# Value steps, page turns and sample scores set between the index pairs of a hybrid decoder layer

## Chip, cores and metric

The kernel runs on one core of one Trainium2 chip. Times are device microseconds of that core. The figure that counts is the median over repeated runs; a profile shows one execution of its own.

## The reference, cut to what matters

One layer of a hybrid model works on a prompt of 1024 tokens and on 8 sample sequences of 4 new tokens each (1056 rows in all, float32). It projects the rows, runs a state-space branch and a sparse attention, mixes both and applies a feed-forward network. The change touches three parts of it:

```
qi, ki, wi : index queries (8 heads of 64), index keys (64), head weights
v          : values (512 columns)
score[t, s] = sum over h of relu(qi[t, h] . ki[s] * 64**-0.5) * wi[t, h] * 8**-0.5
prompt : keys s are the prompt's own 1024 index keys, causal; the 256 best are kept
sample : keys s are 512 past keys from the paged cache (4 pages of 128 rows
         for each of the 8 sequences) and the 4 new ones; the 129 best are kept
```

The first 256 prompt rows keep all their keys, so scores are needed for the prompt's row tiles 2 to 7 and for the sample rows only.

## The kernel before, in words

The program is a sequence of blocks. In a block each engine has its own list of instructions, in an order written out by hand, and they meet through semaphores; a barrier of all engines ends a block. The block in question is the second half of the first one ("s2" semaphores). It ends at 249 us; the block behind it (s3) is called block 3 below.

Projections use float32 numbers split in a high and a low part, with three products each (`split_mm`, L139 to L141). A weight chunk of 1024 x 256 is loaded by SyncE (`load_w`, L199), its high part is written by ScalarE (`split_high`, L205), its low part by GpSimd (`split_low`, L211). There are two chunk buffers, so chunk n+2 can be loaded when the products of chunk n are done. Chunk 5 holds the first 256 value columns, chunk 6 the other 256 (used at the start of block 3), chunk 7 the first gates.

**The index ring.** `UNITS` are the 48 pairs of a row tile i (2 to 7) and a head h. PE works on two units at a time (a pair, 24 in all), one in each half of its rows, over 128 (i + 1) keys (L1016). Their sums go to three slots of two PSUM banks (banks 0 to 5). ScalarE takes each unit through a ReLU into one of two buffers R (L627), VectorE multiplies it with the head's weight and adds it to the tile's scores (L859; the first head of a tile by L854 and L855). A pair may start on PE when the first ReLU of the pair before it is done (`relu_done >= u - 1`); a ReLU waits for the accumulation two units earlier.

**Value columns.** `project_v(n)` computes 128 rows of 256 value columns: 8 steps over the contraction, 3 products each, 24 products in one run. Tile 0 stands ahead of the ring. Tiles 1 to 8 stand behind pairs 2, 4, ..., 16, a whole tile at a time (`FILL`), in banks 6 and 7 by turns. ScalarE copies a tile out (`v_cols`, L617), SyncE stores it.

**Sample scores.** Behind the last pair, PE turns the index pages of one sequence (4 transposes of 128 rows, `pages_T`, L1031), ScalarE or VectorE copies the turned keys and the four new keys to SBUF (L639, L640, L872, L873), and after four sequences PE multiplies them with the sample queries (`sample_units`, L1039); this twice. ScalarE applies the ReLU (L646), PE multiplies with a matrix of head weights that sums over heads (L1052), VectorE copies the scores out (L876, L877).

**SyncE's queue.** All loads and stores are issued by SyncE, in this order: 9 stores of index keys, the load of chunk 5, 32 page loads (L431), the store of the sample head weights (L435), the load of chunk 6, two stores of the state-space kernels (L441), then for each value tile its store (L445) and, for the first four, 8 tiny loads of head weights (L450), the load of chunk 7, and when all index products are done the 8 loads of Uc (L457). Uc is the input of the state-space branch for block 3, 128 partitions x 32 groups x 145 columns, read back from DRAM in rows of 580 bytes; it lies over the index queries `qiT`, which is why it waits for the index products. At its end SyncE waits for the stores of this block, the value stores among them, but not for Uc or weight chunks. PE waits for Uc in block 3, after three value tiles. The first thing that ScalarE does in block 3 is the split of chunk 7.

**ScalarE ahead of the ring** copies the sample queries (L608) and the value tile 0. The split of chunk 6 stands behind unit 20, and GpSimd's part follows it.

Of the kernel before, what the change touches and what calls it, by code (L numbers as in the profile page):

```python
# [17 lines left out]
P = 128  # L18
# [77 lines left out]
def hybrid_kernel(nc, a, outs):  # L96
# [5 lines left out]
    def sem(name):  # L102
        return nc.alloc_semaphore(name=name)
# [181 lines left out]
    qiT = view(36568, 4, T)  # L285
    pg = view(31896, NB, NPG, HD)
    Rb = view(31896, NG, LS)
# [5 lines left out]
    kbT = view(50600, BG, LS)  # L293
# [13 lines left out]
    FILL = [-1] + [5 + 4 * n for n in range(NT - 1)]  # L307
# [5 lines left out]
    with nc.Block() as block:  # L313
# [48 lines left out]
        pT_ev = [sem("s2_pT_ev_act"), sem("s2_pT_ev_dve")]  # L362
        sqk_done = sem("s2_sqk")
        srelu_done = sem("s2_srelu")
# [7 lines left out]
        def _(sp):  # L372
# [55 lines left out]
            for b in range(NB):  # L428
                for j in range(NPG):
                    page = sp.value_load(pt[0:1, b * NPG + j:b * NPG + j + 1], min_val=0, max_val=n_phys - 1)  # L430
                    sp.dma_start(pg[:, b, j, :],  # L431
                                 a["cache_kidx"].rearrange("l n r d -> (l n) r d")[bass.ds(page, 1)]
                                 .rearrange("n r d -> (n r) d")).then_inc(pg_in[b // BG], 16)
            sp.wait_ge(wsc_done, 1)
            sp.dma_start(wi_dram, wsc[0:NB * NS, NT - 1, :]).then_inc(wi_st, 16)  # L435
            sp.wait_ge(mm_done, 15)
            load_w(sp, 6)
            sp.wait_ge(wi_st, 16)
            sp.wait_ge(kern_ev, 10)
            for z in range(2):  # L440
                sp.dma_start(kern_dram[:, GP * z:GP * (z + 1), :],  # L441
                             Kb[32 * z:32 * z + GI].rearrange("i g c -> i g c")).then_inc(kern_st, 16)
            for n in range(NT):
                sp.wait_ge(v_out, n + 1)
# [8 lines left out]
            sp.wait_ge(unit_mm, len(UNITS))  # L453
            sp.wait_ge(qiS_done, 2)
            sp.wait_ge(u_st, 64)
            for t in range(L):
                sp.dma_start(Uc[GI * t:GI * (t + 1), :, :],  # L457
                             u_dram.rearrange("(g i) t c -> t i g c", i=GI)[L - 1 - t]).then_inc(uc_in, 16)
# [34 lines left out]
        def _(act):  # L493
# [113 lines left out]
            for half in range(2):  # L607
                nc.scalar.activation(  # L608
                    qiS[0:64].rearrange("p b (m h) t -> p h m b t", h=2)[:, half],
                    qiT[64 * half:64 * half + 64, :, SEQ:T].rearrange("p m (b t) -> p m b t", t=NS),  # L610
                    ACT.Copy).then_inc(qiS_done, 1)

            def v_cols(n):
                act.wait_ge(v_mm, n + 1)
                if n >= 2:
                    act.wait_ge(v_st[n % 2], 16 * (n // 2))
                nc.scalar.activation(vst1[own(n), n % 2, :], psum[own(n), 6 + n % 2, 0:WC], ACT.Copy).then_inc(v_out, 1)  # L617

            act.wait_ge(tabs, 1)
            v_cols(0)  # L620
            act.wait_ge(kern_ev, 10)
            for u, (i, h) in enumerate(UNITS):
                act.wait_ge(unit_mm, u + 1)
                if u >= 2:
                    act.wait_ge(acc_done, u - 1)
                nk_ = keys_of(i)
                nc.scalar.activation(R[:, u % 2, 0:nk_],  # L627
                                     psum[:, 2 * (u % 3):2 * (u % 3) + 2, :].rearrange("p a b -> p (a b)")[:, 0:nk_],
                                     ACT.Relu, scale=HD ** -0.5).then_inc(relu_done, 1)
                if u == 20:  # L630
                    split_high(act, 6)
                if u in FILL:
                    v_cols(FILL.index(u))
            act.wait_ge(acc_done, len(UNITS))
            for b in range(0, NB, 2):
                act.wait_ge(pT_done, b + 1)
                if b >= BG:
                    act.wait_ge(sqk_done, 1)
                nc.scalar.activation(kbT[0:HD, b % BG, 0:PAST], psum[0:HD, b % 2, :], ACT.Copy)  # L639
                nc.scalar.activation(kbT[0:HD, b % BG, PAST:LS], kiT[0:HD, SEQ + NS * b:SEQ + NS * (b + 1)],  # L640
                                     ACT.Copy).then_inc(pT_ev[0], 1)
                if b == BG + 2:
                    for g in range(NG):
                        act.wait_ge(sqk_done, g + 1)
                        qk = psum[:, 2 + 2 * g:4 + 2 * g, :].rearrange("p a b -> p (a b)")[:, 0:LS]
                        nc.scalar.activation(Rb[:, g, :], qk, ACT.Relu, scale=HD ** -0.5).then_inc(srelu_done, 1)  # L646

        @block.vector
        def _(dve):
# [196 lines left out]
            dve.wait_ge(wsc_done, 1)  # L846
            for u, (i, h) in enumerate(UNITS):
                dve.wait_ge(relu_done, u + 1)
# [11 lines left out]
            dve.wait_ge(wcol_in, 16 * BG * H)  # L860
            for g in range(NG):
                for b in range(BG):
                    rb = slice(HR * b, HR * (b + 1))
                    v.tensor_scalar(wsel[rb, g, NS * (BG * g + b):NS * (BG * g + b + 1)], Et[rb, :], wcol[rb, g:g + 1], None,
                                    ALU.mult).then_inc(sel_done, 1)
            for b in range(1, NB, 2):
                dve.wait_ge(pT_done, b + 1)
                if b == 1:
                    dve.wait_ge(acc_done, len(UNITS))
                if b >= BG:  # L870
                    dve.wait_ge(sqk_done, 1)
                v.tensor_copy(kbT[0:HD, b % BG, 0:PAST], psum[0:HD, b % 2, :])  # L872
                v.tensor_copy(kbT[0:HD, b % BG, PAST:LS], kiT[0:HD, SEQ + NS * b:SEQ + NS * (b + 1)]).then_inc(pT_ev[1], 1)  # L873
            dve.wait_ge(sacc_done, 1)
            ssc = scores(NT - 1)
            link(v.tensor_copy(ssc, psum[0:rs, 6:8, :].rearrange("p a b -> p (a b)")[:, 0:LS]))  # L876
# [3 lines left out]
        def _(pe):  # L880
# [111 lines left out]
            def project_v(n):  # L992
                if n == 0:
                    pe.wait_ge(w_lo_done, 6)
                if n >= 2:
                    pe.wait_ge(v_out, n - 1)
                for k in range(KD):
                    last = split_mm(psum[:, 6 + n % 2, 0:WC], h_parts(k, tok0(n), tok0(n) + P), w_parts(5, k, 0, WC),
                                    k == 0, k == KD - 1)
                last.then_inc(v_mm, 1)  # L1000

            pe.wait_ge(kw_ev, 2)
            project_v(0)
# [3 lines left out]
            for u in range(0, len(UNITS), 2):  # L1007
                i, h = UNITS[u]
                nk_ = keys_of(i)
                if u >= 2:  # L1010
                    pe.wait_ge(relu_done, u - 1)
# [8 lines left out]
                if u + 1 in FILL:  # L1020
                    project_v(FILL.index(u + 1))
            pe.wait_ge(relu_done, len(UNITS))
            pe.wait_ge(v_out, NT)
            pe.wait_ge(qiS_done, 2)

            def pages_T(b):
                pe.wait_ge(pg_in[b // BG], 16 * BG * NPG)
                if b >= 2:
                    pe.wait_ge(pT_ev[b % 2], b // 2)
                for j in range(NPG):  # L1030
                    last = tr(psum[0:HD, b % 2, j * P:(j + 1) * P], pg[:, b, j, :], ident)  # L1031
                last.then_inc(pT_done, 1)

            def sample_units(g):
                for z in range(2):
                    pe.wait_ge(pT_ev[z], BG // 2 * (g + 1))
                for n0, n1 in ((0, 512), (512, LS)):
                    for b in range(BG):
                        last = mm(psum[HR * b:HR * (b + 1), 2 + 2 * g + n0 // 512, 0:n1 - n0],  # L1039
                                  qiS[0:HD, BG * g + b].rearrange("p h t -> p (h t)"), kbT[0:HD, b, n0:n1],  # L1040
                                  start=True, stop=True, tile_position=(0, HR * b))
                last.then_inc(sqk_done, 1)

            for g in range(NG):
                for b in range(BG * g, BG * (g + 1)):
                    pages_T(b)
                sample_units(g)
            pe.wait_ge(sel_done, NB)
            for g in range(NG):
                pe.wait_ge(srelu_done, g + 1)  # L1050
                for n0, n1 in ((0, 512), (512, LS)):
                    last = mm(psum[0:NB * NS, 6 + n0 // 512, 0:n1 - n0], wsel[:, g, :], Rb[:, g, n0:n1],  # L1052
                              start=(g == 0), stop=(g == NG - 1))
            last.then_inc(sacc_done, 1)
# [7 lines left out]
        wcol_in, ki_st, mm_done, ev_done, kw_T, kw_ev, wsc_done, qiS_done, unit_mm, relu_done, acc_done, pT_done, *pT_ev,  # L1062
# [2547 lines left out]
```

## Time and profile before

| | |
|---|---|
| median of 3 runs | 1759.78 us (1758.2 to 1760.35) |
| the profiled execution | 1756.8 us |
| its span | 1755.0 us, mean granted clock 0.981 |
| PE busy | 1646.0 us, 94% |
| VectorE (DVE) busy | 1149.8 us, 66% |
| ScalarE (ACT) busy | 738.5 us, 42% |
| GpSimd (POOL) busy | 641.3 us, 37% |

Shares are of the span. PEld, in the rows, is PE's loading of weights, which overlaps its products. A granted clock of 1.00 is 2.4 GHz, 0.50 is 1.2 GHz. The index ring takes 157 to 231 us of the span, the sample scores 231 to 248. Names such as view_at stand for most tiles, since they are views of one arena; lines tell them apart.

### The profile page before, as it was taken

How to read it: one execution, taken by the hardware profiler on the slowest of the kernel's cores; microseconds unless marked ns; L12 is line 12 of the kernel's file. 1: busy time of each engine (PE TensorE's matmuls, PEld its weight loads, DVE VectorE, ACT ScalarE, POOL GpSimd, SP SyncE). 2: the span in 40 equal slices, each digit the busy share in tenths (PEclk: the TensorE clock that was granted, in tenths of full speed). 3: DMA queues.
4: the chain of work that ended last, by engine and by line, in shares of the span. 5: the costliest groups of instructions: out<-in, count | busy, mean ns of one | idle time of the engine just before them, and what ended most of it. 6: DMA issues, size and time to landing. Idle time of an engine off the chain costs nothing.

```text
span 1755.0 us, 31434 instructions
## 1 busy us (share of the span) xinstructions
PE 1646.0 (94%) x12368; PEld 1510.6 (86%) x12368; DVE 1149.8 (66%) x1946; ACT 738.5 (42%) x1333; POOL 641.3 (37%) x382
## 2 busy tenths in 40 slices
PE   6999879999999998997899999899999999999998
PEld 6997559999999955554699999899999899999998
DVE  5684666998875528872343169565555578998786
ACT  6423547547334435453322335444444433333342
POOL 6121116312212000001544330444444476777792
PEclk9999989999999989999899999999999989999999
DMA  6322151224961114006552433564444464453422
GB/s 164 107 80 59 41 67 53 94 90 119 155 170 40 42 53 146 1 1 201 187 163 90 135 90 107 178 190 166 141 141 145 168 234 160 164 168 135 136 88 99
DMA packets 170197, 209.11 MB, mean 119 GB/s; under 512 B 27410, under 2 KB 114418, under 8 KB 170002
## 3 DMA queue, kind: packets, MB, share of 16 engines
q1 hardware_dynamic: 170050, 207.10, 39.3%
q8 instruction: 98, 1.61, 0.4%
q14 instruction: 49, 0.40, 0.1%
HBM read 148.28 MB, written 58.78 MB: 118 GB/s over the span
## 4 chain that ended last, share of the span: by engine, by line
PE 30%; POOL 9%; DVE 4%; DMA 3%; issue 2%; ACT 2%; SPq 1%; DVEq 0%; ACTq 0%; POOLq 0%
PE psum L139 10%; PE psum L141 10%; PE psum L140 10%; POOL da_lo L3262 5%; DMA view_at<-hid_dram 3%; POOL view_at L3271 1%; ACT da_hi L3138 1%; POOL view_at L3278 1%; POOL view_at L3281 1%; POOL view_at L3274 1%; DVE view_at L3342 1%; SPq L2724 1%; DVE b_lo L3348 1%; PE psum L2863 0%; ACT db_hi L3133 0%
## 5 line engine op out<-in xcount | busy, mean ns | idle before, releaser
L139 PE MATMUL psum<-db_hi,da_hi 128*128 128x264 f32 x896 | 256.6, 286 | 13.9 <-DVE view_at L3458 8.1
L139 PE MATMUL psum<-b_hi,ua_hi 128*128 128x264 f32 x896 | 257.0, 287 | 9.9 <-DVE psum L3406 3.4
L140 PE MATMUL psum<-db_lo,da_hi 128*128 128x264 f32 x896 | 256.4, 286 | 0.0
L141 PE MATMUL psum<-db_hi,da_lo 128*128 128x264 f32 x896 | 256.4, 286 | 0.0
L141 PE MATMUL psum<-b_hi,ua_lo 128*128 128x264 f32 x896 | 256.0, 286 | 0.0
L140 PE MATMUL psum<-b_lo,ua_hi 128*128 128x264 f32 x896 | 255.4, 285 | 0.0
L3258 POOL TENSOR_TENSOR ua_lo<-view_at,ua_hi 128x512 fp32r<-128x512 f32 x99 | 137.3, 1391 | 189.2 <-ACT ua_hi L3067 189.1
L211 POOL TENSOR_TENSOR w_lo<-view_at,w_hi 128x2048 fp32r<-128x2048 f32 (+1 forms) x18 | 81.9, 4548 | 323.7 <-ACT w_hi L205 323.6
L139 PE MATMUL psum<-h_hi,w_hi 128*128 128x352 f32 x600 | 195.1, 325 | 1.3 <-POOL w_lo L211 1.3
L140 PE MATMUL psum<-h_lo,w_hi 128*128 128x352 f32 x600 | 192.7, 321 | 0.0
L141 PE MATMUL psum<-h_hi,w_lo 128*128 128x352 f32 x600 | 192.6, 321 | 0.0
L139 PEld LDWEIGHTS psum<-db_hi,da_hi 128*128 128x128 f32 x896 | 170.2, 190 | 15.9 <-issue 8.5
L3262 POOL TENSOR_TENSOR da_lo<-view_at,da_hi 128x1024 fp32r<-128x1024 f32 x56 | 149.6, 2689 | 93.6 <-ACT da_hi L3138 93.6
L139 PEld LDWEIGHTS psum<-b_hi,ua_hi 128*128 128x128 f32 x896 | 170.0, 190 | 11.2 <-issue 11.1
L141 PEld LDWEIGHTS psum<-b_hi,ua_lo 128*128 128x128 f32 x896 | 170.1, 190 | 0.0
L140 PEld LDWEIGHTS psum<-b_lo,ua_hi 128*128 128x128 f32 x896 | 170.0, 190 | 0.0
L140 PEld LDWEIGHTS psum<-db_lo,da_hi 128*128 128x128 f32 x896 | 169.5, 189 | 0.0
L141 PEld LDWEIGHTS psum<-db_hi,da_lo 128*128 128x128 f32 x896 | 169.4, 189 | 0.0
L3473 DVE TENSOR_TENSOR view_at<-psum,view_at 128x528 f32<-128x528 f32 x204 | 135.7, 698 | 31.9 <-PE psum L141 29.6
L3437 DVE TENSOR_TENSOR db_lo<-view_at,db_hi 128x1056 fp32r<-128x1056 f32 x56 | 118.1, 2108 | 23.1 <-ACT db_hi L3133 22.9
L139 PE MATMUL psum<-w_hi,h_hi 128*128 128x256 f32 x432 | 126.1, 292 | 3.0 <-PEq L1064 2.3
L140 PE MATMUL psum<-w_lo,h_hi 128*128 128x256 f32 x432 | 122.7, 284 | 0.0
(398 smaller groups left out, 3978.2 us busy)
## 6 DMA issues: line engine op xcount, KB each, us to landing
hid_dram<-view_at SPq DMA_DIRECT2D x112, 264.0 KB, 2.1
view_at<-hid_dram SPq DMA_DIRECT2D x56, 528.0 KB, 3.8
view_at<-w_in SPq DMA_DIRECT2D x18, 1024.0 KB, 5.4
view_at<-w_up SPq DMA_DIRECT2D x16, 1024.0 KB, 6.3
view_at<-w_down SPq DMA_DIRECT2D x32, 512.0 KB, 5.7
gate_dram<-view_at SPq DMA_DIRECT2D x48, 176.0 KB, 2.0
view_at<-gate_dram SPq DMA_DIRECT2D x16, 528.0 KB, 4.5
view_at<-cache_k SPq DMA_DIRECT2D x32, 256.0 KB, 3.5
```

The lines of the kernel that those rows point to most:

```text
L139: nc.tensor.matmul(out, lhs[0], rhs[0], start=start, stop=False, skip_group_check=more)
L140: nc.tensor.matmul(out, lhs[0], rhs[1], start=False, stop=False, skip_group_check=more)
L141: return nc.tensor.matmul(out, lhs[1], rhs[0], start=False, stop=stop, skip_group_check=more)
L211: nc.gpsimd.tensor_tensor(w_low[n % 2][:, :, 0:width], w_raw[n % 2][:, :, 0:width], f32(w_high[n % 2][:, :, 0:width]), ALU.subtract).then_ ...
L2724: sp.dma_start(raw_d[d % 2][:, k0::2, cols], w_dn[d][:, k0::2, cols]).then_inc(raw_d_in[j], 16)
L3138: nc.scalar.activation(dah[n % SLOTS], src_d(n), ACT.Copy).then_inc(da_hi, 1)
L3258: tt(slot_u(n)[1], src_u(n), f32(slot_u(n)[0]), ALU.subtract).then_inc(ua_lo, 1)
L3262: tt(dal[n % SLOTS], src_d(n), f32(dah[n % SLOTS]), ALU.subtract).then_inc(da_lo, 1)
L3271: tt(s_d[0], w21, w22, ALU.add).then_inc(sd_done, 1)
L3274: tt(s_d[1], s_d[0], w11, ALU.subtract).then_inc(sd_done, 1)
L3437: v.tensor_tensor(dbl[n % SLOTS], raw_b[n % 3], f32(dbh[n % SLOTS]), ALU.subtract).then_inc(db_lo, 1)
L3473: v.tensor_tensor(two(to), pair(mt), two(to), ALU.add).then_inc(drained, 1)
```

## The change

- Value tiles 1 to 8 are no longer done a tile at a time. Their 64 steps are dealt out behind the pairs: 3, 3, 2 steps in turn behind pairs 0 to 20, then 2, 2, 0 and 4. They use bank 6 alone, so the first step of a tile waits until ScalarE has copied the tile before it.
- The pages of one sequence are turned behind each of pairs 3, 5, ..., 17, in bank 7, and ScalarE alone copies them out, to places that are free during the ring. The order of the sequences is 0, 4, 1, 5, 2, 6, 3, 7. The second of two groups goes to the other half of the partitions.
- The sample units are pair 23 of a ring of 25 pairs: they use the ring's slots and ScalarE's place in it. The four new keys of a sequence are read from `kiT`, not from a copy. The prompt units behind them are shifted by two slots (`ring_of`). The sums over heads follow the last prompt pair. VectorE's eight weight products (`select_weights`) stand ahead of its last two units.
- The page loads of the second group, and ahead of them the store of the sample head weights and the load of chunk 6, change places in SyncE's queue. `split_high(act, 6)` stands ahead of value tile 0; the split in the ring is gone. The sample queries are copied in four instructions.
- Uc is loaded in two parts: groups 0 to 13 when the products of pair 21 are done (they lie over the query heads 0 to 3, which no later pair reads), groups 14 to 31 when the last pair's are. Both parts stand in the queue ahead of the last value tile's store and of the load of chunk 7. Block 3 waits for both.

The diff, cut to its core:

```
+    PB = [g * BG + s for s in range(BG) for g in range(NG)]
-    FILL = [-1] + [5 + 4 * n for n in range(NT - 1)]
+    PAIRS = len(UNITS) // 2 + 1
+    SAMPLE = PAIRS - 2
+        take = (3, 3, 2)[pair % 3] if pair < 21 else (2, 2, 0, 4)[pair - 21]
+    UC_EARLY = 2 * T // UC
+    SUMS = 2 * ((2 * SAMPLE + 1) % 3)
+    PAGE_OF_PAIR = {3 + 2 * n: n for n in range(NB)}
...
 SyncE
-            for b in range(NB):
+            for n, b in enumerate(PB):
+                if n == BG:
+                    sp.wait_ge(wsc_done, 1)
+                    sp.dma_start(wi_dram, wsc[0:NB * NS, NT - 1, :]).then_inc(wi_st, 16)
+                    sp.wait_ge(mm_done, 15)
+                    load_w(sp, 6)
...
             for n in range(NT):
+                if n == NT - 1:
+                    sp.wait_ge(qiS_done, 4)
+                    sp.wait_ge(u_st, 64)
+                    sp.wait_ge(unit_mm, 2 * (SAMPLE - 1))
+                    load_uc(0, UC_EARLY)
+                    sp.wait_ge(unit_mm, 2 * PAIRS)
+                    load_uc(UC_EARLY, G)
                 sp.wait_ge(v_out, n + 1)
                 sp.dma_start(rows(nv, n)[:, 0:WC], vst1[own(n), n % 2, :]).then_inc(v_st[n % 2], 16)
...
             load_w(sp, 7)
-            sp.wait_ge(unit_mm, len(UNITS))
-            for t in range(L):
-                sp.dma_start(Uc[GI * t:GI * (t + 1), :, :],
...
 ScalarE
+            split_high(act, 6)
             act.wait_ge(tabs, 1)
             v_cols(0)
...
-                if u == 20:
-                    split_high(act, 6)
+                for n, k in V_OF_PAIR[pair]:
+                    if k == KD - 1:
+                        v_cols(n)
+                if pair in PAGE_OF_PAIR:
+                    page_out(PAGE_OF_PAIR[pair])
...
 PE
+            def project_v(n, k):
+                if n >= 1 and k == 0:
+                    pe.wait_ge(v_out, n)
...
+            for pair in range(PAIRS):
+                if pair == SAMPLE:
+                    sample_units()
+                else:
+                    prompt_units(2 * pair if pair < SAMPLE else 2 * pair - 2)
+                if pair == PAIRS - 1:
+                    sample_sums()
+                for n, k in V_OF_PAIR[pair]:
+                    project_v(n, k)
+                if pair in PAGE_OF_PAIR:
+                    pages_T(PAGE_OF_PAIR[pair])
...
-            pe.wait_ge(uc_in, 16 * L)
+            pe.wait_ge(uc_in, 2 * 16 * L)
```

## Rows read from the trace of the kernel before

**Rows 1.** Stretches: length, busy us of each engine, granted clock, DMA share, GB/s.
```profile
157.00:231.00 74.00, 58.96 (x356) 36.88 (x355) 47.08 (x54) 39.36 (x58) 4.52 (x1) 1.00 0.17 51
...
230.80:249.10 18.30, 11.53 (x72) 5.79 (x72) 7.30 (x20) 3.83 (x10) 0.00 (x0) 0.72 1.20 115
```

**Rows 2.** PE in order of time: start us, us, line, operation, count [idle before].
```profile
157.06 0.92 PE L1016 MATMUL psum<-view_at,view_at 64*128 64x384 f32 x4
...
160.10 0.92 PE L1016 MATMUL psum<-view_at,view_at 64*128 64x384 f32 x4 [0.57 <-ACT view_at L627]
...
160.94 0.39 PE L139 MATMUL psum<-w_hi,h_hi 128*128 128x256 f32 x1
...
163.98 0.92 PE L1016 MATMUL psum<-view_at,view_at 64*128 64x384 f32 x4
...
190.24 1.56 PE L1016 MATMUL psum<-view_at,view_at 64*128 64x512 f32 x8 [0.79 <-ACT view_at L627]
...
195.03 1.56 PE L1016 MATMUL psum<-view_at,view_at 64*128 64x512 f32 x8 [0.19 <-ACT view_at L627]
...
223.73 1.99 PE L1016 MATMUL psum<-view_at,view_at 64*128 64x512 f32 x8 [1.11 <-ACT view_at L627]
226.82 1.99 PE L1016 MATMUL psum<-view_at,view_at 64*128 64x512 f32 x8 [1.11 <-ACT view_at L627]
```

**Rows 3.** Groups by shape, 157 to 232 us: busy us, mean ns, idle before.
```profile
L859 DVE SCALAR_TENSOR_TENSOR view_at<-view_at,view_at,view_at 128x1024 f32<-128x1024 f32 x7 | 9.0, 1284 | 2.0 <-ACT view_at L627 1.6
...
L627 ACT ACTIVATE view_at<-psum 128x1024 f32<-128x1024 f32 x8 | 7.8, 1021 | 4.7 <-PE psum L1016 4.7
```

**Rows 4.** All engines in order of time, the sample tail and the next block's start.
```profile
230.83 1.06 PE L1031 MATMUL psum<-view_at,view_at 128*64 128x128 f32 x8 [2.02 <-ACT view_at L627]
...
243.81 1.10 PE L1039 MATMUL psum<-view_at,view_at 64*32 64x512 f32 x16 [0.94 <-DVE view_at L873]
...
244.84 2.00 PE L1052 MATMUL psum<-view_at,view_at 128*32 128x512 f32 x8
...
247.60 0.15 DVE L877 TENSOR_TENSOR view_at<-view_at,view_at 32x4 f32<-32x4 f32 x1
...
249.15 1.91 ACT L205 ACTIVATE w_hi<-view_at 128x2048 fp32r<-128x2048 f32 x1 [3.55 <-PEq L1064]
```

**Rows 5.** SyncE's queue in order of time: start us, us of issuing, line, transfer, count.
```profile
150.57 7.99 SPq L431 DMA_DIRECT2D view_at<-cache_kidx  x8
...
228.88 10.25 SPq L457 DMA_DIRECT2D view_at<-u_dram  x8
```

**Rows 6.** Busy time by stretch, just after the next block has started.
```profile
250.00:252.00 2.00, 2.00 (x11) 2.00 (x11) 1.63 (x14) 1.06 (x1) 0.79 (x1) 0.50 0.28 28
```

**Rows 7.** Timeline around a gate store; medians to landing (page, part 6).
```profile
455.89 1.94 SPq L1204 DMA_DIRECT2D gate_dram<-view_at  x1
...
466.93 0.47 ACT L1346 ACTIVATE view_at<-psum 128x352 f32<-128x352 f32 x1 [7.66 <-DMA gate_dram<-view_at]
...
view_at<-w_in SPq DMA_DIRECT2D x18, 1024.0 KB, 5.4
...
gate_dram<-view_at SPq DMA_DIRECT2D x48, 176.0 KB, 2.0
```

**Rows 8.** GpSimd's weight splits and VectorE beside them, in order of time.
```profile
154.11 1.28 DVE L838 COPY view_at<-psum 16x512 f32<-16x512 f32 x2 [0.47 <-PE psum L987]
...
155.42 0.41 DVE L844 TENSOR_TENSOR view_at<-view_at,view_at 16x256 f32<-16x256 f32 x1
...
187.88 4.52 POOL L211 TENSOR_TENSOR w_lo<-view_at,w_hi 128x2048 fp32r<-128x2048 f32 x1 [46.80 <-ACT w_hi L205]
188.43 4.66 DVE L859 SCALAR_TENSOR_TENSOR view_at<-view_at,view_at,view_at 128x640 f32<-128x640 f32 x1 [1.65 <-ACT view_at L627]
...
251.21 4.61 POOL L211 TENSOR_TENSOR w_lo<-view_at,w_hi 128x2048 fp32r<-128x2048 f32 x1 [1.92 <-ACT w_hi L205]
...
253.98 1.14 DVE L1526 TENSOR_SCALAR_CACHE_REDUCE view_at<-view_at,view_at 128x896 bf16<-128x896 f32 x1
```

More of the change, by code:

```diff
@@ L1030, in pages_T @@
                 for j in range(NPG):
-                    last = tr(psum[0:HD, b % 2, j * P:(j + 1) * P], pg[:, b, j, :], ident)
+                    last = tr(psum[0:HD, 7, j * P:(j + 1) * P], pg[:, n, j, :], ident)
                 last.then_inc(pT_done, 1)
[L1034 to L1054, printed above, removed]
+            def sample_units():
+                pe.wait_ge(pT_ev, NB)
+                pe.wait_ge(qiS_done, 4)
+                pe.wait_ge(relu_done, 2 * SAMPLE - 1)
+                for g in range(NG):
+                    half = slice(HD * g, HD * (g + 1))
+                    place = 2 * ((2 * SAMPLE + g) % 3)
+                    for s_ in range(BG):
+                        mm(psum[HR * s_:HR * (s_ + 1), place, :], qiS[half, BG * g + s_].rearrange("p h t -> p (h t)"),
+                           kbT[s_][half, :], start=True, stop=True, tile_position=(HD * g, HR * s_))
+                    for s_ in range(BG):
+                        at_ = SEQ + NS * (BG * g + s_)
+                        last = mm(psum[HR * s_:HR * (s_ + 1), place + 1, 0:NS],
+                                  qiS[half, BG * g + s_].rearrange("p h t -> p (h t)"), kiT[half, at_:at_ + NS],
+                                  start=True, stop=True, tile_position=(HD * g, HR * s_))
+                    last.then_inc(unit_mm, 1)
@@ new lines, in sample_sums @@
+            def sample_sums():
+                pe.wait_ge(sel_done, NB)
+                pe.wait_ge(relu_done, 2 * SAMPLE + 2)
+                for g in range(NG):
+                    for n0, n1 in ((0, PAST), (PAST, LS)):
+                        last = mm(psum[0:NB * NS, SUMS + n0 // PAST, 0:n1 - n0], wsel[:, g, :], Rb[g][:, n0:n1],
+                                  start=(g == 0), stop=(g == NG - 1))
+                last.then_inc(sacc_done, 1)
+            for pair in range(PAIRS):
+                if pair == SAMPLE:
+                    sample_units()
[7 more added lines that the diff above has]
+                    pages_T(PAGE_OF_PAIR[pair])
```

154 lines of the change are left out of this document (72 added, 82 removed).

## The prediction

> **What bounds the kernel now.** Read the busy time by stretch first [rows 1]. The index products run from 157 to 231 us of the span. TensorE (PE) is busy 59.0 of these 74 us, VectorE 47.1, ScalarE 39.4: none is full. The next 18.3 us, in which the sample queries are scored, have PE at 11.5, VectorE at 7.3, ScalarE at 3.8 and a mean granted clock of 0.72: one thing after another, with the engines taking turns. Only the DMA engines are full there (share 1.20, 115 GB/s): the load of Uc.
>
> Then PE's instructions in order of time [rows 2]. A pair of index units without value work costs, with 1024 keys, 226.82 - 223.73 = 3.09 us: products 1.91, then 1.18 in which PE waits for the first ReLU of the same pair (one takes 1.02 [rows 3]). A pair with value work costs the products and 24 value products in one run, 163.98 - 160.94 = 3.04 us. So PE bounds the pairs with value work, the round through ScalarE bounds the others, and the idle 15 us lie in the others. The products hold PE 160.94 - 160.10 = 0.84 us at 384 keys and 0.08 under their busy time at other sizes: 1.56 busy at 768, 1.99 at 1024, so 1.48 and 1.91, and on the same line 1.05, 1.27, 1.69 at 512, 640, 896.
>
> Third, the tail [rows 4]: the last pair starts at 226.82, the first page turn at 230.83, the last VectorE instruction ends at 247.75, the next block starts at 249.15 (1.4 us for the barrier). Last, SyncE's queue [rows 5]: the eight Uc loads are issued from 228.88, when the last index product is done.
>
> **The change part by part.** I follow PE up to the start of the next block, 249.15 before.
>
> 1. Value steps and page turns behind the pairs. The work stays 64 value steps of 3.04 / 8 = 0.38 us, 54 of them in pairs 0 to 19 (20.5 us), 6 in pairs 20 to 22, 4 (1.5 us) behind the last. Products: 4 x (0.84 + 1.05 + 1.27 + 1.48 + 1.69) = 25.3. Eight page turns: two took 1.06 [rows 4], so 0.53 each, plus 0.1 for turning to them and back, 5.0. New are some 13 more turns between products and value steps. A turn is inside the 3.04 already; outside it lies between 0 and the 0.39 that the first value product shows [rows 2]. I take 0.17: 2.2 us. Sum 53.0. Is PE the bound in each? A three-step pair adds 1.31 behind the products, more than the 1.18 of the round at 1024 keys, and the round shrinks with the keys; two steps (0.93) fall short only at 768 keys, by under 0.1. VectorE needs 2.6 us a pair at 1024 keys (1.28 each [rows 3]), never the bound. Pairs 20 to 22 have two steps: 2.8 us of PE under the round of 3.09, so 9.3.
>
> 2. Sample units as pair 23. One group of four took 1.10 us at full clock [rows 4]; two, 2.2. The eight small weight products of VectorE and two ReLUs of 516 keys stand under it and the next pair. What goes is the chain of page turn, copy, turn, copy in the tail. The last prompt pair starts at 157.06 + 53.0 + 9.3 + 2.2 = 221.6, before at 226.82.
>
> 3. Behind it: products 1.99, sums 2.00 [rows 4], four value steps 1.5: PE is done 5.5 us later. VectorE: products 2.0, one ReLU 1.0, two accumulations 2.6, two small ones about 0.9 (estimate), with semaphores 6.7 us later. By engines alone the next block could start at 221.6 + 6.7 + 1.4 = 229.7, 19.5 us sooner.
>
> 4. The Uc loads, in two halves. SyncE now issues 14 of 32 groups after pair 21 and 18 after the last pair; behind them stand the last value store, then the load of chunk 7, and then the wait for all value stores that ends the block. Before, no store of this block was left when Uc was issued. The eight loads of before ran at full DMA from 228.88 until about 250.5 (115 GB/s up to 249.1 [rows 1], share 0.28 over 250 to 252 [rows 6]): 21.6 us. Bytes and row sizes stay. Pair 21 starts at 157.06 + 53.0 + 3.1 = 213.2, its products end at 215.2, the data end at 236.8 whether or not the second half is late by some tenths. The store must wait for that: in block 3 the gate store issued at 455.89, behind loads of the same kind, let ScalarE go on only at 466.93, 11 us, where the median gate store lands in 2.0 [rows 7]. So store at 237.3, barrier 1.4, next block at 238.8 (rounded). **The tail's new end is the DMA queue, not an engine, and it gives back 9 of the 19.5 us.** Bounds of this wait: none (start 229.7), or, with the store taking the 2.0 us of a free gate store after the last data, 240; the second half, issued at 1.28 us a load as before [rows 5], is out by 234 and adds nothing.
>
> 5. Chunk 6 earlier. Its load goes between the first and second 16 page loads: the last eight took 8.0 us and the last one ends at 158.6 [rows 5], so the load is issued about 142, when the query products allow it, and lands after the 5.4 us of the median weight load [rows 7], 147.9. ScalarE splits it in 1.9 [rows 4] while idle, GpSimd from 150 to 154.6. Before, GpSimd's split at 187.88 stretched a 640-key accumulation to 4.66 us, where 1024 keys take 1.28 [rows 3, 8]; but value products stood beside it, and the pair of 190.24 took 4.79 instead of 1.48 + 3.04: it cost 0.3 us, in my sum by the new pairs. At the new place VectorE makes copies out of PSUM until 155.4, then products of two SBUF tensors from 155.42 [rows 8]. Price 0; if the load lands 1 us late, up to 1 us on the first ReLU.
> In block 3 an instruction with one SBUF tensor, 896 keys, took 1.14 us inside a GpSimd split of 4.61 [rows 8], which is its plain length; the one with two waited. The Trainium skill, page "SBUF — State Buffer", section "Who interferes with whom", says the same as a rule: VectorE contends with a GpSimd read of SBUF only with two SBUF inputs or in a two-port mode, and the later one blocks fully. By it the copies from PSUM pass and the price is 0; without it the rival of the lock, below.
>
> 6. Chunk 7's load, which before stood ahead of Uc and now stands behind it. It lands near 236.8 + 5.4 = 242.2, 3.4 us into the block, whose first ScalarE instruction splits it. PE first makes three value tiles of about 3 us each into banks of their own, and uses chunk 7 far later. Price 0, bound 2. ScalarE's four smaller query copies instead of two, the second sum bank and the semaphores: 0, all before 157 or off PE's order.
>
> 7. Clock. Before, PE ran at 1.2 GHz up to past 252 [rows 6], having been idle from 246.8 [rows 4]. Now it idles 11 us: the same again, between 1.5 us gained and 2 lost; I take 0.
>
> Sum: 249.2 - 238.8 = 10.4 us, and what follows shifts as a whole. The profiled execution took 1756.8 us (span 1755.0): 1746.4. The median of the runs is 3.0 above it, and the forecast is for that median: 1759.8 - 10.4 = **1749.4**.
>
> **The rivals.**
> - The store isn't held by the queue, or Uc drains faster beside idle engines. Gain 15 to 19.5, the rest taken back by ScalarE waiting for chunk 7. About 1743. Against it the 11 us of [rows 7].
> - The ring doesn't speed up. A turn costs 0.39 instead of 0.17 (2.9 us), and the single value bank makes PE wait for ScalarE's copy at eight tile ends, up to 0.5 each (4 in all; now two banks alternate). All of it moves Uc's start too. Gain 3.5 to 7; about 1755. For it: PE is the bound, so nothing hides it. Against: the copy has the next pair's products (0.84 us or more) as cover.
> - The lock: any VectorE instruction blocks beside GpSimd's split at 150 to 154.6. The kernel copies end 4 us late, the first ReLU 3 us late: 1752.5.
> - Slower: load time goes by transfers, not bytes. Eight loads took 21.6 us, 2.7 each; sixteen at 2.7 are 43 us from 215.2, the block starts at 260, 11 us later: 1771. It decides from 2.0 us a load on (32 us). For it: the queue is the new end, and it is twice as many transfers with the same destination rows. Against: the DMA share of 1.20 says that the engines move data all the time, not that the queue starts and stops.
>
> **How the numbers follow.** Forecast 0.62; store free 0.10; ring no faster 0.17; lock 0.05; sixteen slow loads 0.05; rest, as a low clock in the ring, 0.01. Under 0.2% (3.5 us) no change can be told here. Faster: forecast, store free, lock, and some 0.11 of the ring case, 0.88; within 0.2%: 0.06; slower: 0.06. The range takes the store case at its near end and the ring case: 1743 to 1755.
>
> **What would show it.** Right: PE nearly without idle time from 157 to 210, the last prompt pair near 221.6, SyncE's first Uc load near 215, VectorE's last instruction near 228.3 and then some 10 us in which only DMA is busy, next block near 239. GpSimd's split ends before 155.4 and no accumulation in the ring is stretched. Wrong: the block starting within 2 us of VectorE's last instruction (part 4); the last pair after 224 (part 1); PE waiting for ScalarE's value copies; Uc loads still running past 240; PE waiting in the next block for Uc or for ScalarE.

## The result, and the profile after

Four runs of the changed kernel took 1741.14 to 1747.76 us, median 1746.94; four of the kernel before, on the same chip, 1755.78 to 1760.35, median 1758.99. The medians lie 12.05 us apart, where 10.4 was forecast. The recorded ratio, which is not the quotient of these two medians, is 0.9942 (0.9922 to 0.9963); by it the gain is 10.2 us (6.5 to 13.7). The profiled execution took 1741.14 us (span 1739.3).

The starts of the two kernels differ: the changed kernel's mean granted clock from 10 to 50 us was 0.83, the other's 1.00, and its first index product starts at 158.13 instead of 157.06. The change did not make this: the same kernel, profiled once more, had a clock of 1.00 there and started its index products at 157.08. So below a time "from the ring" is counted from the first index product, and the forecast's times are taken so too (less 157.06).

Busy time by stretch, with the columns of [rows 1]: the ring up to the last index products, then the hole behind it, then the first 10 us of block 3.

```profile
158.13:222.90 64.77, 63.39 (x403) 39.85 (x404) 42.74 (x56) 39.94 (x64) 0.00 (x0) 1.00 0.22 37
...
231.50:239.40 7.90, 0.00 (x0) 0.00 (x0) 0.00 (x0) 0.00 (x0) 0.00 (x0) 0.50 1.16 188
...
240.00:250.00 10.00, 10.00 (x69) 10.00 (x68) 9.34 (x39) 2.68 (x3) 4.60 (x1) 0.76 0.08 27
```

PE is now busy 63.4 of the ring's 64.8 us. Then comes a stretch in which no engine does anything and the DMA share is 1.16. PE in order of time shows the pairs, as [rows 2]:

```profile
158.13 0.92 PE L1041 MATMUL psum<-view_at,view_at 64*128 64x384 f32 x4
...
160.25 0.92 PE L1041 MATMUL psum<-view_at,view_at 64*128 64x384 f32 x4
...
210.33 1.99 PE L1041 MATMUL psum<-view_at,view_at 64*128 64x512 f32 x8
...
213.42 1.99 PE L1041 MATMUL psum<-view_at,view_at 64*128 64x512 f32 x8 [0.20 <-ACT view_at L668]
...
219.71 1.12 PE L1063 MATMUL psum<-view_at,view_at 64*32 64x512 f32 x16 [0.30 <-ACT view_at L668]
...
221.55 1.99 PE L1041 MATMUL psum<-view_at,view_at 64*128 64x512 f32 x8 [0.68 <-ACT view_at L662]
...
224.24 2.01 PE L1077 MATMUL psum<-view_at,view_at 128*32 128x512 f32 x8 [0.70 <-DVE view_at L880]
```

Pair 0, with three steps, takes 160.25 - 158.13 = 2.12 us, and no wait stands before the next pair's products, where [rows 2] had one of 0.57. Pair 20, the first one in this list with 1024 keys, takes 3.09, with a wait of 0.20 in it: two steps do not fill the round, as the forecast had it. SyncE's queue in order of time, as [rows 5]:

```profile
142.83 0.40 SPq L199 DMA_DIRECT2D view_at<-w_in  x1
143.98 17.07 SPq L451 DMA_DIRECT2D view_at<-cache_kidx  x16
...
215.54 13.35 SPq L461 DMA_DIRECT2D view_at<-u_dram  x16
...
228.93 0.45 SPq L473 DMA_DIRECT2D out<-view_at  x1
229.42 0.43 SPq L199 DMA_DIRECT2D view_at<-w_in  x1
```

The last value store (L473) is issued at 228.93, at once behind the sixteen Uc loads, ahead of chunk 7, as the forecast had it. What SyncE itself waited for behind it (source line waited at, releaser, total us, times, longest):

```profile
SPq L486 <- DMA out<-view_at: 8.0, 1, 8.0
```

L486 is the wait for the value stores at the block's end. It begins when chunk 7 is issued (229.85), so it ends near 237.9. The last VectorE instruction and the start of block 3, as [rows 4]:

```profile
227.93 0.15 DVE L901 TENSOR_TENSOR view_at<-view_at,view_at 32x4 f32<-32x4 f32 x1
...
239.46 0.55 PE L139 MATMUL psum<-w_hi,h_hi 128*128 128x256 f32 x1 [11.61 <-PEq L1101]
...
240.60 1.91 ACT L205 ACTIVATE w_hi<-view_at 128x2048 fp32r<-128x2048 f32 x1 [12.33 <-DMA view_at<-w_in]
```

L1101 is the barrier. What filled the 11.4 us is in the DMA rows of 214 to 245 us, 40 slices of 0.775 us, busy share in tenths and GB/s:

```profile
DMA  0136999999999799999999999999999991000000
GB/s 0 45 124 141 186 124 128 114 118 125 124 111 121 84 181 108 121 118 124 107 130 103 130 104 130 108 124 119 136 190 334 346 349 58 0 0 0 0 11 0
```

From the slice that begins at 215.5 up to about 236.2 the DMA engines move some 120 GB/s, which is mostly Uc, and from 217 on they are full in nearly every slice; the three slices at 334 to 349 GB/s behind it are the long rows of chunk 7, until 239.6.

### The profile page after: what moved, and what is told of

It is laid out like the page before. It is cut to its first block, busy times and chain, and to the rows that moved or that the text cites. A ratio compares the mean times of both kernels' runs of the same rounds, so it can differ in the third digit from the quotient of the medians.

```text
span 1739.3 us, 31423 instructions
## 1 busy us (share of the span) xinstructions
PE 1643.9 (95%) x12368; PEld 1510.0 (87%) x12368; DVE 1143.5 (66%) x1938; ACT 740.4 (43%) x1335; POOL 637.9 (37%) x382
## 4 chain that ended last, share of the span: by engine, by line
PE 30%; POOL 9%; DVE 4%; DMA 3%; issue 2%; ACT 2%; SPq 1%; DVEq 0%; ACTq 0%; POOLq 0%
PE psum L139 10%; PE psum L141 10%; PE psum L140 10%; POOL da_lo L3299 5%; DMA view_at<-hid_dram 3%; POOL view_at L3308 1%; ACT da_hi L3175 1%; POOL view_at L3318 1%; POOL view_at L3315 1%; POOL view_at L3311 1%; SPq L2761 1%; DVE view_at L3379 1%; DVE b_lo L3385 1%; DVE view_at L3510 0%; PE psum L2900 0%
## 5 line engine op out<-in xcount | busy, mean ns | idle before, releaser
L211 POOL TENSOR_TENSOR w_lo<-view_at,w_hi 128x2048 fp32r<-128x2048 f32 (+1 forms) x18 | 81.7, 4538 | 283.5 <-ACT w_hi L205 283.4
L139 PE MATMUL psum<-w_hi,h_hi 128*128 128x256 f32 x432 | 128.2, 297 | 12.3 <-PEq L1101 11.6
```

The costliest lines, as they stand in the source:

```text
L139: nc.tensor.matmul(out, lhs[0], rhs[0], start=start, stop=False, skip_group_check=more)
L211: nc.gpsimd.tensor_tensor(w_low[n % 2][:, :, 0:width], w_raw[n % 2][:, :, 0:width], f32(w_high[n % 2][:, :, 0:width]), ALU.subtract).then_ ...
```

## The experiments

Every kernel is the changed one with the edit shown, cut to its core; "store ahead, split late", "split third" and "chunk ahead" contain the edit of "store ahead" too, and show what comes on top. Times from the ring, in us, of one profiled execution each; medians and ratios are of the runs beside the kernel before on the same chip (its median was 1756.44 us beside "store ahead", "store ahead, split late", "Uc as before" and "whole tiles", and 1757.68 beside the other four). The columns are starts: of block 3; in it, of the products that read Uc, and of the Y stage, which is PE's first product with the matrix M for the output of the state-space branch; and of GpSimd's first weight split in the down-projection at the end of the kernel. "Last" is the time from that split to the last one, in which no kernel differs from another.

```
kernel                    block 3  Uc products  Y stage  first down  last   median    ratio (95%)
                                                         split
before                      92.0      102.2      315.8    1233.9    323.9  1758.99    1
changed                     81.3       92.3      304.1    1221.9    317.3  1746.94   0.9942 (0.9922 to 0.9963)
changed, once more          81.7       92.0      303.8    1220.3    319.9  1741.74   0.9926 (0.9902 to 0.9951)
store ahead                 72.2       82.3      301.2    1218.1    320.7  1739.7    0.9896 (0.9854 to 0.9937)
store ahead, split late     72.1       82.3      304.5    1221.4    322.3  1743.14   0.9921 (0.9899 to 0.9944)
store ahead, split third    72.3       83.4      298.4    1219.7    320.5  1738.64   0.9880 (0.9858 to 0.9902)
chunk ahead                 73.8       84.4      297.3    1215.7    324.0  1737.85   0.9883 (0.9866 to 0.9899)
Uc as before                86.1       98.5      311.5    1230.0    321.1  1749.36   0.9961 (0.9944 to 0.9978)
whole tiles                 89.7      101.0      311.1    1227.2    321.0  1751.36   0.9969 (0.9950 to 0.9988)
split in the ring           86.0       97.2      308.9    1225.9    320.7  1748.1    0.9955 (0.9934 to 0.9977)
```

**Store ahead.** Is the 11 us hole the store's wait behind Uc, or the barrier itself? The last four steps go behind pairs 21 to 23, so the last store can be issued before the second half of Uc.

```
-        take = (3, 3, 2)[pair % 3] if pair < 21 else (2, 2, 0, 4)[pair - 21]
+        take = (3, 3, 2)[pair % 3] if pair < 21 else (3, 3, 2, 0)[pair - 21]
...
-                    sp.wait_ge(unit_mm, 2 * PAIRS)
-                    load_uc(UC_EARLY, G)
                 sp.wait_ge(v_out, n + 1)
                 sp.dma_start(rows(nv, n)[:, 0:WC], ...)
+            sp.wait_ge(unit_mm, 2 * PAIRS)
+            load_uc(UC_EARLY, G)
             load_w(sp, 7)
```

> The changed kernel with the last eight value steps dealt 3, 3, 2, 0 behind pairs 21 to 24 (it had 2, 2, 0, 4), so that the last value tile is done before the last pair, and its store issued ahead of the second half of the Uc loads. Same work, same transfers. Lengths are counted from the first index product to the first instruction of block 3; the changed kernel's is 81.3 us, that of the kernel before 92.1. Theory (the block's end waits for the store that is queued behind Uc): 73 us (+-1.5), the time by engines alone, some 8 us less; the Uc data still end 78 us after the first index product, inside block 3, so there ScalarE waits for chunk 7 (queued behind Uc) up to 10 us into the block and gives 1 to 3 us back: total 5 to 7 us under the changed kernel. Rival (the block's end is set by something else, as SyncE's time to issue 16 loads, or the Uc data themselves): 79 to 81 us and no gain in total.

The queue, the end of VectorE and block 3's start in this kernel, in order of time:

```profile
222.53 0.33 SPq L471 DMA_DIRECT2D out<-view_at  x1
...
223.88 4.39 SPq L461 DMA_DIRECT2D view_at<-u_dram  x8
...
228.20 0.15 DVE L901 TENSOR_TENSOR view_at<-view_at,view_at 32x4 f32<-32x4 f32 x1
...
230.40 0.36 PE L139 MATMUL psum<-w_hi,h_hi 128*128 128x256 f32 x1 [4.04 <-PEq L1101]
...
241.86 1.91 ACT L205 ACTIVATE w_hi<-view_at 128x2048 fp32r<-128x2048 f32 x1 [16.08 <-DMA view_at<-w_in]
```

Block 3 starts 2.1 us behind VectorE's last instruction, 9.1 us sooner than in the changed kernel, and SyncE no longer waits at the value stores: the hole was the store's. But only 2.9 of the 9.1 are left at the Y stage; I had expected to lose 1 to 3, and 6.2 are gone. ScalarE's first instruction of block 3 waits for chunk 7, which now is wanted early and lands at 241.9. The time moved from a wait of all engines to a wait of ScalarE, which everything behind it in its order shares.

**Store ahead, split late.** If that wait eats the rest, ScalarE should copy the three value tiles and the twelve banks of the Uc products first and split chunk 7 behind them.

```
-            split_high(act, 7)
             for n in range(VA):
                 take_v(n)
...
+            split_high(act, 7)
             act.wait_ge(mm_done, I0 + 1)
```

> As store_ahead, and in block 3 ScalarE splits chunk 7 after it has taken the three first value tiles and the twelve state-space banks, instead of first. Theory: length to block 3 again 73 us, and the whole of the 8 us stays: PE waits for neither Uc nor ScalarE in the first 30 us of block 3. Total 7 to 9 us under the changed kernel, 1738 to 1741 for the median. Rival (the late chunk costs nothing, since ScalarE has slack): the same time as store_ahead within 1 us.

A miss: no gain, and the Y stage 3.3 us later than with the split first. GpSimd's half of the split went with ScalarE's, and behind it on GpSimd stand rotations that VectorE needs. VectorE and GpSimd in the next part of the block:

```profile
304.71 4.59 POOL L211 TENSOR_TENSOR w_lo<-view_at,w_hi 128x2048 fp32r<-128x2048 f32 x1
304.86 5.53 DVE L1577 TENSOR_TENSOR view_at<-view_at,view_at 128x1024 f32<-128x1024 f32 x1 [5.77 <-POOL view_at L1328]
```

In "store ahead" the same instruction starts at 301.57, without a wait, and takes 1.23 us. From the ring it now starts 2.2 us later (145.6 for 143.4). Then 4.3 us more go, since it has two SBUF inputs and stands beside GpSimd's next split (304.71 to 309.30); in "store ahead" that split came at 306.74, behind it. "Split in the ring", below, shows the same clash. The edit moved an instruction on two engines, and only one of them had been looked at.

**Store ahead, split third.** The split goes between the second and third copy, so GpSimd is late by less.

```
+            for n in range(2):
+                take_v(n)
             split_high(act, 7)
-            for n in range(VA):
-                take_v(n)
+            take_v(2)
```

> As store_ahead, and in block 3 ScalarE copies two value tiles out before it splits chunk 7, then the third. Theory: chunk 7 lands about 11.5 us into the block, so ScalarE is behind by 2 us instead of 4 when the state-space banks come; PE waits under 1 us; state-space products end at 93 us from the first index product, and GpSimd's chain is no later than in the changed kernel, unlike with the split behind all banks. Median 1739 (+-2). Rival: as store_ahead, 94.8.

ScalarE waited 2.41 us for chunk 7 instead of standing at it from the start:

```profile
240.13 1.91 ACT L205 ACTIVATE w_hi<-view_at 128x2048 fp32r<-128x2048 f32 x1 [2.41 <-DMA view_at<-w_in]
```

The Y stage starts at 298.4, 2.8 sooner than in "store ahead", but at the down-projection nothing of that is left (1219.7 against 1218.1); what took it in between was not followed up. The medians of the two (1738.64 and 1739.7) are not to be told apart.

**Chunk ahead.** The other cure: chunk 7 is loaded before the second half of Uc, which is wanted 10 us later in block 3.

```
+            load_w(sp, 7)
             sp.wait_ge(unit_mm, 2 * PAIRS)
             load_uc(UC_EARLY, G)
-            load_w(sp, 7)
```

> As store_ahead (last value tile done before the last pair, its store ahead of the second half of Uc), and the load of chunk 7 goes out ahead of that half too, as soon as the value products are done. Lengths from the first index product. Theory (each wait follows the order of one queue): block 3 at 72.2 us as in store_ahead; ScalarE splits chunk 7 at once in block 3 (it waited 11.5 us into the block for it in store_ahead); the second half of Uc ends near 84 us, and PE wants it at 82.3, so PE waits 1 to 2 us for Uc instead. State-space products end at 92 (store_ahead 94.8, changed 100.1), value-score stage of block 3 (first product of M) 6 us sooner than changed. Median 1739 (+-2). Rival (what store_ahead lost in block 3 was not the chunk): state-space products end at 94 to 95 as in store_ahead.

```profile
221.90 0.43 SPq L199 DMA_DIRECT2D view_at<-w_in  x1
222.88 6.51 SPq L461 DMA_DIRECT2D view_at<-u_dram  x8
...
230.98 0.16 POOL L1296 MEMSET view_at<- 128x32 f32 x1 [76.49 <-POOLq L1101]
...
230.99 1.91 ACT L205 ACTIVATE w_hi<-view_at 128x2048 fp32r<-128x2048 f32 x1 [6.21 <-PEq L1101]
```

ScalarE splits as soon as the block starts. The price is 1.6 us at the block's start, because SyncE now needs 6.51 us instead of 4.39 to issue eight loads (the queue ahead of it is fuller) and reaches the barrier later. At the Y stage it is 6.8 us ahead of the changed kernel (6 was expected), and its ratio, 0.9883 (0.9866 to 0.9899), lies below that of the changed kernel run beside it, 0.9926 (0.9902 to 0.9951), with 0.0003 between the intervals. Its down-projection starts soonest of all, at 1215.7. With "split third" it has the lowest ratio here, and both beat the changed kernel: the four runs of each (up to 1740.64 and 1740.77) lie below all nine of the changed one (1740.93 to 1751.54), though the intervals of the ratios only touch for "split third". The two are not to be told apart.

**Uc as before.** What is Uc's early first half worth? Eight whole loads, behind the last index product, the last store and chunk 7.

```
-                if n == NT - 1:
-                    ...
-                    load_uc(0, UC_EARLY)
-                    sp.wait_ge(unit_mm, 2 * PAIRS)
-                    load_uc(UC_EARLY, G)
...
             load_w(sp, 7)
+            sp.wait_ge(unit_mm, 2 * PAIRS)
+            sp.wait_ge(qiS_done, 4)
+            sp.wait_ge(u_st, 64)
+            load_uc(0, G)
```

> The changed kernel with the Uc loads as they were: eight whole loads, after the last index product, behind the last value store and the load of chunk 7. The ring and the sample units stay as changed. Theory (queue order): the store is free, so block 3 starts 72 to 73.5 us after the first index product, 8 us sooner than changed; but Uc's 20 us of data start only after the chunk, near 234 us, and end near 254, where PE wants them some 12 us into block 3 (243): PE waits about 11 us there. Total 2 to 4 us slower than the changed kernel. Rival (Uc is hidden anyway, as in the kernel before): 8 us faster than the changed kernel.

```profile
227.47 0.43 SPq L199 DMA_DIRECT2D view_at<-w_in  x1
228.00 13.43 SPq L461 DMA_DIRECT2D view_at<-u_dram  x8
...
243.02 0.15 POOL L1293 MEMSET view_at<- 128x32 f32 x1 [88.79 <-POOLq L1098]
```

A miss by 13 us at the block's start. I had freed the barrier of the store, but SyncE itself must have issued its loads before it can join the barrier, and behind 1 MB of chunk 7 the eight Uc loads took 13.43 us to issue, 1.68 each. Against the changed kernel block 3 is 4.8 us later and the Y stage 7.4, although no store waits behind Uc here. This is not the worth of the early first half alone, since chunk 7 ahead of Uc and the whole loads keep SyncE longer. "Chunk ahead" comes nearer to it, with chunk 7 ahead of the second half and no store behind it either: against it block 3 is 12.3 us later, the Y stage 14.2 and the median 11.5. These two still differ in whole loads against halves and in where the last value steps stand.

**Whole tiles.** The value work tile by tile behind every second pair, as the old scheme, but with all else as changed.

```
-        take = (3, 3, 2)[pair % 3] if pair < 21 else (2, 2, 0, 4)[pair - 21]
+        take = 8 if pair in range(2, 17, 2) else 0
```

> The changed kernel with the value tiles dealt as before, eight steps behind each of pairs 2, 4, ..., 16, page turns, sample pair and queue as changed. Theory (the ring was bound by the ScalarE round in pairs without value work and by PE in the others, and spreading fills the first): from the first index product to the start of the last prompt pair 71 to 72 us where the changed kernel has 63.4, and the same 8 us later in everything behind; total 7 to 9 us slower than changed. Rival (the gain is the tail's alone, spreading only moves value work): within 2 us of the changed kernel.

The ring of this kernel, in the columns of [rows 1]:

```profile
157.40:231.20 73.80, 64.67 (x417) 40.56 (x416) 43.62 (x60) 40.84 (x65) 0.00 (x0) 0.99 0.21 34
```

PE is busy 64.7 us, 1.3 more than in the changed kernel, but idle 9.1 instead of 1.4 (the 1.3 are a last pair that ran in part at 1.2 GHz). The last prompt pair starts 71.4 us from the ring (228.81) instead of 63.4. Dealing out the steps is worth 8 us in the ring, as expected. Of these 7.0 are left at the Y stage, 5.3 at the down-projection and 4.4 between the medians (1751.36 and 1746.94), where I had expected 7 to 9; where they went was not followed up.

**Split in the ring.** Chunk 6's split in the middle of the ring, as before.

```
-            split_high(act, 6)
             act.wait_ge(tabs, 1)
...
+                if pair == 10:
+                    split_high(act, 6)
                 for n, k in V_OF_PAIR[pair]:
```

> The changed kernel with chunk 6's split back in the ring, behind pair 10 (its load stays early). Theory (with two SBUF inputs VectorE is shut out while GpSimd reads SBUF, and in the new ring PE's slack behind the accumulations is under 1 us): one accumulation of 640 keys takes 4.5 us or more, PE waits for ScalarE 1.5 to 3 us at the next pairs, ScalarE's 1.9 us of its own delays one ReLU; from the first index product to the last prompt pair 65.5 to 67.5 us instead of 63.4, total 2 to 4 us slower than changed. Rival (it was hidden before and is hidden now): 63.4 to 63.9.

```profile
184.84 4.53 POOL L211 TENSOR_TENSOR w_lo<-view_at,w_hi 128x2048 fp32r<-128x2048 f32 x1 [44.15 <-ACT w_hi L205]
185.38 5.65 DVE L898 SCALAR_TENSOR_TENSOR view_at<-view_at,view_at,view_at 128x640 f32<-128x640 f32 x2 [1.25 <-ACT view_at L667]
...
190.14 0.81 ACT L667 ACTIVATE view_at<-psum 128x768 f32<-128x768 f32 x1 [3.46 <-DVE view_at L898]
...
191.00 2.51 PE L1042 MATMUL psum<-view_at,view_at 64*128 64x512 f32 x6 [2.76 <-ACT view_at L667]
```

The four us behind it, in the columns of [rows 1]:

```profile
191.00:195.00 4.00, 4.00 (x17) 2.32 (x18) 2.00 (x5) 1.84 (x3) 0.00 (x0) 0.65 0.00 0
```

Two accumulations that take 0.88 us each elsewhere take 5.65 together: the first stands until GpSimd's split is done at 189.37. ScalarE waits 3.46 for VectorE, PE 2.76 for ScalarE, and the last pair starts 4.3 us later (67.7 from the ring, just above the 65.5 to 67.5 expected). The wait is not all of it: the pair at 191.00 starts 2.9 us later from the ring than its like in the changed kernel, and after PE's idle time it has a mean granted clock of 0.65, so it takes 4.6 us instead of 3.2, which is the other 1.4. The prediction had priced the old stall at 0.3 us, rightly for the kernel before, where PE had 24 value products to do beside it. With PE as the bound there is no such cover, and the moved split is part of the gain: 4.1 us at the down-projection, while the medians are 1.2 apart (6.4 from the repetition's).

**Changed, once more**, beside "split third", "chunk ahead" and "split in the ring":

> The changed kernel once more, beside the others. Both theories: block 3 at 81.3 us from the first index product within 0.3, the last stage of the kernel (down-projection), whose length differed by 6.6 us between the two first profiles while nothing of it was changed, anywhere between these two; median 1745 to 1748. If the 15.7 us between the first two profiles' spans were the change's own, the profile here would show a last stage as short as in the first profile of the changed kernel.

Block 3 and the Y stage fall within 0.4 us of the first profile; its five runs spread over 10.6 us, 1740.93 to 1751.54. Their median, 1741.74, misses the 1745 to 1748 expected and lies 5.2 us below that of the first four runs of the same kernel. So some 5 us between two medians can come from the runs alone, and the positions are the better measure.

## Why the prediction was right

By the steps of the prediction, from the ring:

1. **Pairs 0 to 19** took 210.33 - 158.13 = 52.2 us, forecast 53.0; pairs 20 to 22 took 9.38 (forecast 9.3). The turns between products and steps, a term of 2.2 us for which no row of before had a price, cost some 1.4 if the other terms hold. The single value bank cost little: the weight loads' waits for ScalarE's value copies are 1.8 us in three places, and PE as a whole was idle for 1.4 us of the ring. The ring rival falls, and "whole tiles" shows the mechanism with 8 us.

2. **The sample pair** took 221.55 - 219.71 = 1.84 us, forecast 2.2; 0.68 of it is a wait for the first of its two ReLUs.

3. **By engines** VectorE ends at 228.08, from the ring 69.95, where the forecast's 228.3 is 71.2. Most of that is the last pair's start, 63.4 for 64.5.

4. **The queue** decides, as forecast. First Uc load 57.4 from the ring (forecast 58.1), last data about 78.1 (79.7), block 3 at 81.3 (81.7). "Store ahead" takes the store away from behind the loads and gets block 3 at 72.2 (by engines alone 72.6 was worked out). The price of the wait, 9.1 us by that run, was read off one gate store in [rows 7]. The 0.5 us given to the store itself had no row: the last Uc load landed at 237.8 and SyncE's wait for the stores ended near 237.9, then the barrier took 1.5. One thing in this step was off and did no harm: the sixteen smaller loads were issued in 13.35 us, not 20; the second eight took 5.29, 0.66 each. The rival of the sixteen slow loads falls: 2,320 KB in 20.7 us is the rate of before. The Trainium skill, page "DMA: Bandwidth & Descriptors", section "Two DMAs through the same engine are not ordered", says that within one queue of one DMA engine descriptors start in order, which is no promise on the order in which their writes end. The trace agrees as far as it can show it: a 32 KB store issued at 228.93 let the barrier go only when the 20 us of loads before it were through. That a small store lands behind the loads is this case's measurement.

5. **Chunk 6's split** stood beside copies out of PSUM:

```profile
148.97 1.91 ACT L205 ACTIVATE w_hi<-view_at 128x2048 fp32r<-128x2048 f32 x1
...
150.96 4.52 POOL L211 TENSOR_TENSOR w_lo<-view_at,w_hi 128x2048 fp32r<-128x2048 f32 x1 [8.80 <-ACT w_hi L205]
151.69 1.28 DVE L865 COPY view_at<-psum 16x512 f32<-16x512 f32 x2 [0.40 <-PE psum L1011]
153.44 1.28 DVE L865 COPY view_at<-psum 16x512 f32<-16x512 f32 x2 [0.47 <-PE psum L1011]
...
156.49 0.41 DVE L871 TENSOR_TENSOR view_at<-view_at,view_at 16x256 f32<-16x256 f32 x1
```

The copies take 1.28 us a pair as in [rows 8], inside GpSimd's 4.52. The first instruction with two SBUF inputs comes a microsecond after it. The lock rival falls for this place, and "split in the ring" shows the lock at the other. The rule that the prediction took from the Trainium skill (page "SBUF — State Buffer", section "Who interferes with whom") agrees with both traces. That split's old place, priced at 0.3 us, is the one value of this step that holds only for the kernel before.

6. **Chunk 7** landed at 240.6, from the ring 82.5 where 85.1 was forecast, and ScalarE waited only 1.2 us into the block. Nothing on PE's path waited for it.

7. **The clock** was taken as 0. PE ran at 1.2 GHz for the first 5.3 us of block 3 (239.46 to 244.72) against 3.3 before (249.17 to 252.50), 1.0 us lost, inside the stated bounds of 1.5 gained to 2 lost. So 10.7 at the block's start are 9.9 at the Uc products.

What was not in the sum is what came after. Up to the Y stage 9.9 became 11.7. In the kernel before, ScalarE waited 21.1 us in all for gate stores, in the changed one 16.0. Only before did PE wait ahead of the Y stage, 1.6 us. That wait ended at 472.8, when the last load that the Y stage reads (from `u_dram`, issued at 463.04) had just landed, at 472.65; in the changed kernel the same load landed at 458.79, 3.2 us before PE came to it. So it was this load and not a gate store that PE waited for, though both stand in SyncE's queue. The waits of the two, their total in us, times, and the longest:

```profile
ACT view_at L1346 <- DMA gate_dram<-view_at: 21.1, 8, 7.7
```

```profile
ACT view_at L1383 <- DMA gate_dram<-view_at: 16.0, 8, 6.5
```

Then a short stretch of the kernel before was granted the lower clock, where the changed one's neighbourhood was not; the columns are those of [rows 1]:

```profile
474.50:478.00 3.50, 3.50 (x20) 2.74 (x21) 3.40 (x4) 0.46 (x1) 0.00 (x0) 0.54 0.95 269
```

```profile
455.00:475.00 20.00, 20.00 (x163) 17.47 (x163) 19.33 (x20) 6.07 (x11) 4.80 (x1) 1.00 0.41 113
```

A stretch of 3.4 us at 1.2 GHz costs 1.7 us. None of the nine profiles of the other kernels has a low clock there, but with one profile of the kernel before it is not shown that the change took it away. The load and the clock are not in the forecast's sum. The two profiled spans differ by more than the medians, 15.7 us: 12.0 up to the down-projection's first split, less the 1.1 by which the ring started later, 6.6 in the last stage, which is the same code, and 1.9 lost behind it. Over the ten profiles that stage varied from 317.3 to 324.0, and from 317.3 to 319.9 between the two of the changed kernel, so its 6.6 us are not counted as part of the gain. The median of four runs, 12.05 less, agrees with the 12.0 of the positions. That agreement, and how near the forecast of 1749.4 came to 1746.94, are partly luck: in the repetition the positions give 13.6 and the medians 15.9, and its median of 1741.74 lies below the forecast's range of 1743 to 1755. All nine runs together have a median of 1745.86. What held in both profiles is the steps, up to the start of block 3.

## What to carry to other kernels

A barrier ends when the last thing in front of it has landed, and here a small store landed behind the loads that had been issued before it on the same queue: issue the stores that a barrier waits for ahead of the bulk loads that it does not (here 9 us at the block's start). When such a wait goes, look at once at what else stood in its shadow; of the 9 us two thirds were gone at the Y stage while ScalarE waited for chunk 7, until that load was issued earlier. When an instruction is moved, look at every engine that it feeds. And a stall that costs nothing while another engine has slack (GpSimd's split, 0.3 us) costs nearly its whole length once PE is the bound: 2.9 us of waiting, and 1.4 more at the lower clock that followed.

## What the runs showed of the hardware

- SyncE's time to issue a load followed what was still under way, not the instruction. Eight Uc loads took 10.25 us on a short queue with whole parts [rows 5], 3.74 to 4.39 us in halves on a short queue, 5.29 in halves behind other halves, 6.51 behind 1 MB, and 13.43 whole behind 1 MB. In both kernels with whole loads the last three were issued only as the first three landed: before at 233.98, 236.57 and 239.13 against landings at 233.90, 236.59 and 239.24, and in "Uc as before" at 236.09, 238.77 and 241.44 against 236.21, 238.95 and 241.72. SyncE can't join a barrier while it issues, which made "Uc as before" 13 us later than I expected.
- GpSimd's split (4.5 us) and VectorE: copies out of PSUM beside it kept their 1.28 us for two, an accumulation with more than one SBUF input stood until the split had ended (5.65 us for two of 0.88).
- The last stage, with the same code in ten profiles, took 317.3 to 324.0 us. That is more than half of the gain that was to be measured, so what a change brings is better read from positions in the trace than from two spans.
